# Dilated projections in a tuned decoder layer: a second group by seven products for the k half, and two weight sums of each group made by accumulating DMAs

## The reference, cut to what matters

```python
x = x + 0.5 * swiglu(rmsnorm(x, ffn1_norm), ...)
h = rmsnorm(x, mix_norm)
proj = h @ w_in            # 256 x 2048 by 2048 x 10248
q_d, k_d, v_d, q_f, k_f, v_f, f_logit, g_d, g_f = jnp.split(proj, split_points, axis=-1)
qa = partial_rope(split_heads(q_d)) * scale
ka = partial_rope(split_heads(k_d))
y_dil = dilated_attention(qa, ka, split_heads(v_d))
y_fox = forgetting_attention(q_f, k_f, v_f, log_f)
...                        # gated merge, w_out, a second swiglu, a last rmsnorm
```

## Time and profile before

| | before |
|---|---|
| device time, median of 3 | 2041.95 us (2041.85 to 2042.55) |
| profiled execution, span from first to last instruction | 2040.2 us |
| PE busy | 2027.8 us, 99% |
| DVE busy | 1858.9 us, 91% |
| ACT busy | 1267.5 us, 62% |
| POOL busy | 87.6 us, 4% |

### The profile page before, as it was taken

How to read it: one execution, slowest core, us unless ns; L and a number is a source line. 1 busy time by engine, 2 the same in 40 slices (tenths; PEclk the granted TensorE clock), 3 DMA queues, 4 the chain that set the end, 5 groups by cost and what they waited for, 6 DMA issues and landing times.

```text
span 2040.2 us, 26364 instructions
## 1 busy us (share of the span) xinstructions
PE 2027.8 (99%) x9204; PEld 1678.7 (82%) x9204; DVE 1858.9 (91%) x1897; ACT 1267.5 (62%) x1474; POOL 87.6 (4%) x80
## 2 busy tenths in 40 slices
PE   9999999999999999999999999999999999999998
PEld 7888888888888888888888888888888888888886
DVE  7999999999999798887689999799999999999997
ACT  7666666666666556666556556466666666666664
POOL 0000000000000000000000000000000000000000
PEclk9999999999999999999999999999999999999999
DMA  8578777787877455554536575655878777877773
GB/s 301 206 211 259 230 236 246 227 236 227 246 247 235 157 186 183 198 177 157 183 134 227 189 243 182 211 186 192 242 223 250 244 232 211 260 225 240 247 231 127
DMA packets 222143, 441.03 MB, mean 216 GB/s; under 512 B 7648, under 2 KB 7824, under 8 KB 221936
## 3 DMA queue, kind: packets, MB, share of 16 engines
q1 hardware_dynamic: 202112, 401.64, 56.1%
q0 software_dynamic: 19744, 38.28, 11.3%
q10 hardware_dynamic: 208, 0.08, 0.0%
HBM read 400.13 MB, written 2.10 MB: 197 GB/s over the span
## 4 chain that ended last, share of the span: by engine, by line
PE 98%; DVE 1%; ACT 0%; DMA 0%; issue 0%; SPq 0%; ACTq 0%; DVEq 0%
PE ps L765 16%; PE ps L767 16%; PE ps L766 16%; PE ps L778 12%; PE ps L780 12%; PE ps L779 12%; PE ps L1002 2%; PE ps L1003 2%; PE ps L1001 2%; PE ps L1050 2%; PE ps L1052 2%; PE ps L1051 2%; PE ps L856 1%; PE ps L834 0%; DMA xres<-in_x 0%; PE ps L1169 0%
## 5 line engine op out<-in xcount | busy, mean ns | idle before, releaser
L1788 DVE TENSOR_TENSOR w_lo<-raw,w_hi 128x1024 fp32r<-128x1024 f32 x280 | 337.9, 1219 | 7.2 <-ACT w_hi L1356 4.9
L1356 ACT ACTIVATE w_hi<-raw 128x1024 fp32r<-128x1024 f32 x280 | 290.8, 1053 | 72.6 <-PE ps L767 54.0
L1356 ACT ACTIVATE w_hi<-sums 128x1024 fp32r<-128x1024 f32 x160 | 169.8, 1063 | 204.8 <-PE ps L767 71.4
L1788 DVE TENSOR_TENSOR w_lo<-sums,w_hi 128x1024 fp32r<-128x1024 f32 x160 | 195.3, 1222 | 33.8 <-ACT w_hi L1356 31.1
L765 PE MATMUL ps<-w_hi,hT_hi 128*128 128x512 f32 x536 | 208.8, 390 | 0.0
L767 PE MATMUL ps<-w_hi,hT_lo 128*128 128x512 f32 x536 | 208.5, 389 | 0.0
L766 PE MATMUL ps<-w_lo,hT_hi 128*128 128x512 f32 x536 | 208.5, 389 | 0.0
L1788 DVE TENSOR_TENSOR more_lo<-raw,more_hi 128x1024 fp32r<-128x1024 f32 x140 | 169.2, 1219 | 6.6 <-ACT more_hi L1356 5.6
L765 PE MATMUL ps<-w_hi,xT_hi 128*128 128x512 f32 x424 | 170.1, 401 | 0.0
L1356 ACT ACTIVATE more_hi<-raw 128x1024 fp32r<-128x1024 f32 x140 | 146.4, 1054 | 32.6 <-PE ps L767 23.8
L767 PE MATMUL ps<-w_hi,xT_lo 128*128 128x512 f32 x424 | 165.7, 391 | 0.0
(11 more groups left out here) (366 smaller groups left out, 5007.4 us busy)
## 6 DMA issues: line engine op xcount, KB each, us to landing
raw<-in_ffn_w_up SPq DMA_DIRECT2D x88, 1024.0 KB, 5.5
raw<-in_ffn_w_down SPq DMA_DIRECT2D x88, 1024.0 KB, 5.3
raw<-in_ffn_w_gate SPq DMA_DIRECT2D x87, 1024.0 KB, 5.4
raw<-in_w_in SPq DMA_DIRECT2D x80, 1024.0 KB, 5.0
xres<-gate_buf POOLq DMA_DIRECT2D x72, 512.0 KB, 5.5
raw<-in_w_out SPq DMA_DIRECT2D x16, 1024.0 KB, 5.1
raw<-in_w_proj_dil SPq DMA_DIRECT2D x8, 1024.0 KB, 5.5
raw<-in_w_proj_fox SPq DMA_DIRECT2D x8, 1024.0 KB, 5.2
```

What stands on the lines that cost most here:

```text
L1356: nc.scalar.activation(slot_hi(place, offset), src, ACT.Copy).then_inc(hi_ready, 1)
L1788: nc.vector.tensor_tensor(slot_lo(place, offset), step_source(r)[0], slot_hi(place, offset).bitcast(F32), ALU.subtract).then_inc(lo_ready, 1)
```

## The change

It has three parts. (1) Pair 1 takes the 22-slab form with two groups by seven, which only the v pair had. (2) In all eight groups by seven DVE makes two sums, T3 and T2, and POOL issues two accumulating DMAs of 512 KB that make T1 in place in the up block and T4 in place in the gate block; signs of tokens and sums are turned so that only additions are needed. The order of the seven slabs changes so that the two come last. (3) The frees of buffers, the waits, the places of two combining adds and the slabs after which pair 1 transposes follow from that.

```diff
-D_SLABS, D_LOADS = (19, 19, 22, 19, 19, 19), 8
+D_SLABS, D_LOADS = (19, 22, 22, 19, 19, 19), 8
...
-D_SEVEN, D_GATE, D_UP = zip(_QK, _QK, _V, _QK, _QK, _QK)
-
-_QK_FREE, _V_FREE = (-6, -4, -2, 0, 2, 4, 6, 11), (-6, -4, -2, 0, 2, 7, 9, 11)
-D_FREE = (_QK_FREE, _QK_FREE, _V_FREE, _QK_FREE, _QK_FREE, _QK_FREE)
-
-D_SUMS, D_COMBINED = (0, 4, 8, 16, 20, 24), 5
+D_SEVEN, D_GATE, D_UP = zip(_QK, _V, _V, _QK, _QK, _QK)
+
+_QK_FREE, _V_FREE = (-6, -4, -2, 0, 2, 4, 6, 12), (-6, -4, -2, 0, 2, 8, 9, 11)
+_AFTER_V = (-5,)
+D_FREE = (_QK_FREE, _V_FREE, _AFTER_V + _V_FREE[1:], _AFTER_V + _QK_FREE[1:], _QK_FREE, _QK_FREE)
...
+D_PRODUCTS = (("gate", 1), ("sum", T3), ("sum", T2), ("gate", 0), ("up", 1), ("sum", T1), ("sum", T4))
...
-    DIL_TURNS = ((), (0, 1, 3, 4), (0, 1, 4, 6), (), (), ())
+    DIL_TURNS = ((), (0, 1, 4, 6), (0, 1, 4, 6), (), (), ())
...
-                if l is None:
-                    act.wait_ge(dil_summed, D_SUMS[c] + 4 * which + PRODUCTS[o][1] + 1)
+                part, seven = D_PRODUCTS[o][1] if kind == "paired" else None, D_BEFORE[c] + which
+                if l is None and part in (T1, T4):
+                    added_by = dil_t1_added if part == T1 else dil_t4_added
+                    act.wait_ge(added_by[seven % 2], (seven // 2 + 1) * 16)
...
+            def dil_add(c, s):
...
+                pool.wait_ge(dil_summed, 2 * seven + 1)
+                pool.wait_ge(raw_landed[gate_l % LOADS], place.landed(gate_l))
+                pool.dma_start(up[:, 0::2, :], gate[:, 0::2, :], accum_op=ALU.add)\
+                    .then_inc(dil_t1_added[seven % 2], 16)
+                pool.wait_ge(dil_summed, 2 * seven + 2)
+                pool.wait_ge(lo_ready, place.slab(first + 1))
+                pool.dma_start(gate[:, 1::2, :], dil_sums_at(c, T2), accum_op=ALU.add)\
+                    .then_inc(dil_t4_added[seven % 2], 16)
...
-                if kind == "paired" and o in (1, 2, 4):
-                    dil_sum(c, which, {1: T1, 2: T2, 4: T4}[o])
+                if kind == "paired" and o == 0:
+                    dil_sum(c, which, T2)
...
-                if r == last + 4:
+                if r == last + 5:
                     dve.wait_ge(dil_m1_copied, c + 1)
...
                 if r == last + 6:
+                    dve.wait_ge(slab_done, place.slab(last + 6))
```

More of the change, by code:

```diff
@@ L409, in dil_sums_at @@
     def dil_sums_at(c, which):
+        place = int(which == T2)
         if c < F_PAIR:
-            return dil_sums[:, SUM_PLACE[which]]
-        return v_sb[:, SUM_PLACE[which], D_MIX:2 * D_MIX].rearrange("p (a b) -> p a b", b=CH)
+            return dil_sums[:, place]
+        return v_sb[:, place, D_MIX:2 * D_MIX].rearrange("p (a b) -> p a b", b=CH)
     def dil_source(e):
@@ L418, in dil_source @@
         if kind == "paired":
-            what, part = PRODUCTS[o]
+            what, part = D_PRODUCTS[o]
+            up_l, gate_l = D_SEVEN[c][which][2]
+            if what == "sum" and part in (T3, T2):
+                return dil_sums_at(c, part), None
             if what == "sum":
-                return dil_sums_at(c, part), None
-            l = D_SEVEN[c][which][2][what == "gate"]
+                return raw[:, (up_l if part == T1 else gate_l) % LOADS, (part == T4)::2, :], None
+            l = gate_l if what == "gate" else up_l
             return raw[:, l % LOADS, part::2, :], l
@@ L466, in build @@
     dil_summed = sem("dil_summed")
+    dil_t1_added = [sem(f"dil_t1_added{n}") for n in range(2)]
+    dil_t4_added = [sem(f"dil_t4_added{n}") for n in range(2)]
     dil_m1_copied = sem("dil_m1_copied")
@@ L1644, in _ @@
                     attend(DIL_SLOTS[c, r], 0)
-                if r == last + 3:
-                    act.wait_ge(slab_done, place.slab(last + 2))
+                if r == last + 4:
+                    act.wait_ge(slab_done, place.slab(last + 4))
                     parts = partial if c < F_PAIR else fox_partial
@@ L1728, in _, with add_down @@
             pool.memset(f_abs[0:1, 0, 0:1], 0.0).then_inc(down_copied, 2)
-            for j in range(2 * (STEPS - 1)):
+            def add_down(j):
                 for n in range(NN):
@@ L1735, in _ @@
                                    accum_op=ALU.add).then_inc(down_added[n], 16)
+            def dil_add(c, s):
+                place, (first, group, (up_l, gate_l)), seven = dil_place(c), D_SEVEN[c][s], D_BEFORE[c] + s
+                up, gate = raw[:, up_l % LOADS], raw[:, gate_l % LOADS]
+                pool.wait_ge(dil_summed, 2 * seven + 1)
[6 more added lines that the diff above has]
+                    .then_inc(dil_t4_added[seven % 2], 16)
+            for j in range(STEPS - 1):
+                add_down(j)
+            for c in range(D_PAIRS):
+                for s in range(D_SEVENS[c]):
+                    dil_add(c, s)
+            for j in range(STEPS - 1, 2 * (STEPS - 1)):
+                add_down(j)
         @block.vector
@@ L2094, in dil_sum @@
                 up, gate = raw[:, up_l % LOADS], raw[:, gate_l % LOADS]
-                done = D_SUMS[c] + 4 * s
-                out = dil_sums_at(c, which)
+                seven = D_BEFORE[c] + s
                 if which == T3:
-                    dve.wait_ge(lo_ready, place.slab(at - 2))
+                    if s > 0:
+                        dve.wait_ge(lo_ready, place.slab(D_SEVEN[c][s - 1][0] + 2))
                     dve.wait_ge(raw_landed[up_l % LOADS], place.landed(up_l))
-                    made = nc.vector.tensor_tensor(out, up[:, 1::2, :], up[:, 0::2, :], ALU.subtract)
-                if which == T1:
-                    dve.wait_ge(lo_ready, place.slab(at - 1))
-                    dve.wait_ge(raw_landed[gate_l % LOADS], place.landed(gate_l))
[L2104 to L2112, removed]
+                    made = nc.vector.tensor_tensor(dil_sums_at(c, T3), up[:, 1::2, :], up[:, 0::2, :], ALU.add)
+                else:
+                    if seven > 0:
+                        dve.wait_ge(dil_t4_added[(seven - 1) % 2], ((seven - 1) // 2 + 1) * 16)
+                    if s > 0:
+                        dve.wait_ge(lo_ready, place.slab(D_SEVEN[c][s - 1][0] + 3))
+                    dve.wait_ge(raw_landed[gate_l % LOADS], place.landed(gate_l))
+                    dve.wait_ge(dil_summed, 2 * seven + 1)
+                    made = nc.vector.tensor_tensor(dil_sums_at(c, T2), dil_sums_at(c, T3), gate[:, 0::2, :],
+                                                   ALU.add)
                 made.then_inc(dil_summed, 1)
```

21 lines of the change are left out of this document (13 added, 8 removed).

## The result

| | before | after |
|---|---|---|
| device time, median | 2042.08 us (2041.84 to 2042.55, 7 runs) | 2046.86 us (2046.38 to 2049.28, 7 runs) |
| profiled execution, span | 2040.2 us | 2044.7 us |
| profiled execution, device time | 2041.95 us | 2046.69 us |

What follows compares the result with a forecast made beforehand. PE was taken as the bound, filling 270.0 of 270.0 us of the dilated stage. -1.36 + 1.7 + 0.4 = +0.7 us on the 2040.2 span gives 2040.9, plus 1.75 outside it: 2042.7 us, range 2040.4 to 2046.8.

Steps and rivals of the forecast that it cites:

- The matmuls, -1.36: Pair 1 swaps a plain group for a group by seven: 6 PE matmuls fewer at 0.2267 us, 1.36 us less.
- The wait at the end of pair 0, +0.4: T3 and T2 of the next pair come ahead of DVE's up add, so PE's transposes wait 0.4 us.
- The wait at the end of pair 1, +1.7: PE waits 1.7 us after slab 0 of pair 2 for DVE's turning of q's second half.
- The accumulating DMAs, 0: In the second groups by seven of pairs 1 and 2, POOL's DMAs land in time: no PE wait, 0 us.
- The rule for when PE waits: In the tight groups PE waits the larger of L - 7.6 and L + A - 13.3 us, if above 0.
- L: Time the gate load (load 5) of a tight group takes, with a median of 5.3 us.
- A: Time from T4's issue to its landing in a tight group, with a median of 5.5 us.
- The rival with late operands: Slow loads and adds in the tight groups make PE wait 2.6 us twice: 2047.9 us, 9 in 100.
- DVE as the hidden limit: Rival: the 10.2 us of work taken off DVE come through, giving 2031 us; 2 in 100.

Runs made afterwards that it cites:

- both edits: Changed kernel with turned tiles of pairs 1 and 2 transposed one slab later and their load 7 freed at slab 15, not 11: 2040.82 us, again 2041.13.
- load 7 later: Changed kernel with load 7 of pairs 1 and 2 freed at slab 15 instead of 11: 2042.76 us.
- the pair alone: Kernel before with pair 1 in the 22-slab form and all 32 sums made by DVE, no accumulating DMA in the stage: 2044.72 us.
- T4 by DVE: Changed kernel with DVE adding T2 onto gate odd itself in place of T4's accumulating DMA, T1 still a DMA: 2045.02 us.
- load 7 at 13: Changed kernel with load 7 of pairs 1 and 2 freed at slab 13 instead of 11: 2048.50 us.
- turns one slab later: Changed kernel with the first half of the turned tiles in pairs 1 and 2 transposed after slab 1 of the next pair, and so on: 2043.12 us.

## Why the prediction was wrong

**The matmuls, -1.36: right.** The version with both edits has no wait in the stage and is 1.5 us under before from the stage's first matmul on, 1.0 to 1.2 in the medians.

**The wait at the end of pair 0, +0.4: right,** 0.35 measured.

**The wait at the end of pair 1, +1.7: right as worked out (1.8 with load 7 later), and 2.34 in the change.** The template, the third pair of the kernel before, has T4 in time; here T4 was late and the run behind it started later. One number of the working is a slip without effect on the sum: by its own terms DVE gets to the up add at 837.6 and is done with it at 838.7, so it has 0.5 us and not 1.6 to spare against PE's last slab. In the pair alone that margin was used up.

**The accumulating DMAs, 0: this step failed.** The rule for when PE waits was 0.4 to 0.7 us too kind, and L was right (5.2, taken as 5.3). A was taken as 5.5, the median of 72 DMAs of the feed-forward part, and the four DMAs of the tight groups took 8.9 to 9.0. It cost 0.30 + 1.10 + 1.05 us of direct waits, and 0.5 more at the turning: 3.0 us, against 0. With -1.36, 0.35, 1.8 and 3.0 the sum is +3.8, and the traces show +3.7 and +3.9. The most in the earlier trace rows was 9.0, so the value that came true was in the shown rows; the fault was to choose the median of a population without asking what lies beside the DMA. The rival with late operands was this mechanism, at 9 in 100; its L + A of 15.9 was also too much, 14.1 being measured.

**Why load 7.** The prediction looked at load 7 of the q, k pairs, whose free was moved by one slab. The rival with late operands names loads 6 and 7 beside T1 and T4, but takes no price from them. In the v form load 7 is issued at slab 11, on top of T1, and this entry of the table the change left alone. Before, no accumulating DMA was in flight there: the same entry, a new neighbour.

**The shared engines.** The prediction put beside its first rival the section Issuing engines are not separate DMA queues, of the page DMA: Bandwidth & Descriptors of the Trainium skill: DMAs of all engines share the 16 DMA engines. By it POOL's adds and SP's loads slow each other. The runs agree, 5.5 us for T1 of pair 1 without load 7 beside it against 8.9 to 9.0 with it, and this was the rule to give more weight.

**DVE as the hidden limit: wrong, as forecast.** DVE has 8.8 us less work (10.2 were worked out) and PE's spacing is 0.227 us as before; PE waits for single late instructions of DVE, not for its sum.

**What the change would need.** The expected gain of the six matmuls is there, and is eaten by waits that come from two numbers of the tables. With both moved the kernel is at 2040.8 and 2041.1 us, the best of all that were run.

## What to carry to other kernels

The time of a DMA is not a property of the DMA. When one is put on a path with little slack, list every transfer that is in flight at that moment, and take the duration from a row with the same neighbours, or the worst one shown. A large prefetch whose data isn't wanted yet may go a few slabs later for nothing: here four slabs did, and two made it worse. And work out a wait with the late case as well: one late operand moved the next wait by 0.5 us.

## What was not expected of the hardware

**An accumulating DMA and a load slow each other by half and more.** Load 7 of pair 1 takes 5.1 us in the pair alone, where no add is in the stage, and 6.4 to 7.9 where T1 or T4 moves beside it for most of its time. In the tight groups T1 (512 KB) takes 5.0 to 5.5 us where load 7 is issued 3 us or more behind it, and 7.9 to 9.2 where it is issued at the same time or up to 1.0 us ahead. The place matters: T4 took 9.7 and 10.0 us with the load 0.6 us behind it.

**A wait of PE can cost more than its own length.** Behind waits that cost 2.1 to 2.8 us the granted clock was at its lower level, 1.2 GHz and not 2.4, for seven or eight matmuls in three of the profiled executions (T4 by DVE, load 7 at 13, the pair alone the third time), with steps of 0.43 us instead of 0.227, which added 1.4 to 1.6 us. In T4 by DVE the granted clock reads 0.50 from 799.8 to 803. In four others with a wait of 2.3 to 2.4 us for the turning (the change twice, the pair alone twice) it did not fall, and behind waits of 1.8 us and less no fall was seen. What decides it is open. It fits the two groups of runs of the pair alone; it does not explain all scatter, for turns one slab later, with no wait above 0.9 us in its profile, spreads over 2.5 us too.
